# Two transformer blocks on one core: the GEMM units beside a stage's end split by token halves, and weights in half-MB pieces

## The reference

```python
def rmsnorm_2(x, g):
    y = xf * lax.rsqrt(jnp.mean(xf * xf, axis=-1, keepdims=True) + RMS_EPS)
    return (y * g.astype(jnp.float32)).astype(x.dtype)
...
for i in range(DEPTH_2):
    mod = c_act @ ada_w[i] + ada_b[i]
    sh1, sc1, g1, sh2, sc2, g2 = jnp.split(mod, 6, axis=-1)
    h = modulate(rmsnorm_2(x, norm_gain[i, 0]), sh1, sc1)
    y = mixer(h)          # swa, gla or fox, by i
    x = x + g1[:, None, :] * y
    h = modulate(rmsnorm_2(x, norm_gain[i, 1]), sh2, sc2)
    x = x + g2[:, None, :] * swiglu(h, ffn_w_gu[i], ffn_w_down[i])
```

## Time and profile before

| | |
|---|---|
| time, median of 3 runs | 2488.33 us (2488.05 to 2489.48) |
| the profiled execution | 2488.01 us |
| its span, first to last instruction | 2486.2 us |
| PE, DVE, ACT busy | 2277.7, 1615.7, 1097.2 us |
| mean granted clock of PE | 0.956 |
| read from memory | 450.30 MB, mean 184 GB/s |

### The profile page before, as it was taken

One profiled execution on the slowest core, in us unless ns is written; L12 is line 12 of the kernel. 1 busy time (PEld: TensorE's weight loads), 2 busy tenths in 40 slices (PEclk: granted clock), 3 DMA queues, 4 the chain that ended last, 5 costly groups with the idle time before them and its releaser, 6 DMA issues. The chain is left out here.

```text
span 2486.2 us, 34298 instructions
## 1 busy us (share of the span) xinstructions
PE 2277.7 (92%) x14225; PEld 2033.1 (82%) x14225; DVE 1615.7 (65%) x2293; ACT 1097.2 (44%) x1769; POOL 180.0 (7%) x183
## 2 busy tenths in 40 slices
PE   6999998989999998877999897999899999878998
PEld 6998886879988877756999775899786899757997
DVE  4676678656766785576888476777546555565554
ACT  4454445434444454444343442444444444444443
POOL 0000001010000011000000022000000000100000
PEclk8999999999999999878999998999998999988999
DMA  8866655556666654333899441587531465422551
GB/s 278 276 222 222 225 193 182 206 198 225 220 217 216 220 203 155 123 119 125 286 314 325 143 126 61 190 287 272 174 102 34 140 195 186 142 71 91 184 186 49
DMA packets 291919, 458.82 MB, mean 185 GB/s; under 512 B 10912, under 2 KB 158858, under 8 KB 291764
## 3 DMA queue, kind: packets, MB, share of 16 engines
q1 hardware_dynamic: 285796, 439.62, 52.5%
q0 software_dynamic: 5968, 17.02, 2.4%
HBM read 450.30 MB, written 6.29 MB: 184 GB/s over the span
## 5 line engine op out<-in xcount | busy, mean ns | idle before, releaser
L147 DVE TENSOR_TENSOR wlo<-raw,whi 128x1024 fp32r<-128x1024 f32 x640 | 775.0, 1236 | 405.9 <-ACT whi L141 404.4
L141 ACT ACTIVATE whi<-raw 128x1024 fp32r<-128x1024 f32 x640 | 662.2, 1055 | 532.0 <-PE G L135 496.1
L135 PE MATMUL G<-HTh,whi 128*128 128x256 f32 x2432 | 699.5, 288 | 6.8 <-DVE wlo L147 2.0
L135 PE MATMUL G<-HTl,whi 128*128 128x256 f32 x2432 | 690.0, 284 | 0.0
L135 PE MATMUL G<-HTh,wlo 128*128 128x256 f32 x2432 | 689.9, 284 | 0.0
L135 PEld LDWEIGHTS G<-HTh,whi 128*128 128x128 f32 x2432 | 468.4, 193 | 13.5 <-issue 7.4
L135 PEld LDWEIGHTS G<-HTl,whi 128*128 128x128 f32 x2432 | 468.5, 193 | 2.2
L135 PEld LDWEIGHTS G<-HTh,wlo 128*128 128x128 f32 x2432 | 468.2, 193 | 0.0
L135 PE MATMUL G<-whi,HTh 128*128 128x512 f32 (+1 forms) x704 | 278.3, 395 | 5.5 <-DVE pool L147 5.1
L155 DVE SCALAR_TENSOR_TENSOR pool<-raw,c,pool 128x512 f32<-128x512 f32 x336 | 267.9, 797 | 10.2
L135 PE MATMUL G<-wlo,HTh 128*128 128x512 f32 (+1 forms) x704 | 268.8, 382 | 0.0
(11 more groups left out here) (150 smaller groups left out, 2577.7 us busy)
## 6 DMA issues: line engine op xcount, KB each, us to landing
raw<-in_ada_w SPq DMA_DIRECT2D x96, 1024.0 KB, 5.9
raw<-in_ffn_w_gu SPq DMA_DIRECT2D x176, 512.0 KB, 4.9
raw<-in_w_in SPq DMA_DIRECT2D x112, 512.0 KB, 4.6
raw<-in_w_in SPq DMA_DIRECT2D x48, 1024.0 KB, 5.1
raw<-in_ffn_w_down SPq DMA_DIRECT2D x44, 1024.0 KB, 5.0
raw<-in_swa_w_in SPq DMA_DIRECT2D x12, 1024.0 KB, 5.2
raw<-in_gla_w_in SPq DMA_DIRECT2D x12, 1024.0 KB, 6.5
raw<-in_fox_w_in SPq DMA_DIRECT2D x12, 1024.0 KB, 5.3
```

The costliest lines, as they stand in the source:

```text
L135: return self.e.matmul(out, a, b, start=start, stop=stop, skip_group_check=True) if self.e else self
L141: return self.e.activation(out, a, func, bias=bias, scale=scale, accum_out=accum) if self.e else self
L147: return self.e.tensor_tensor(out, a, b, op) if self.e else self
```

## The change

The unit before each turn from one stage to the next, and the first unit of the next stage, are computed one token half after the other (`Apart`, six matmuls of 512 columns a step), and `turn` writes out their order: the first half of the last unit, its second half but for the last step, norm and transposes of the first half around that step, three steps of the next unit, norm and transposes of the second half around the fourth, then its second half. At the end of the FFN the last two down products take the place of the last unit. The scaling by the norm is applied to the rows on ACT (`rows`), and the transposes are plain; they go 4 blocks of 128 columns at a time, with four affine instructions of 128. The mean and power are made for each half, without the division by the width; the gains carry its root (32) instead. The first unit of each stage is one whose tokens are stationary (V first in the dilated, gla and fox stages), and the FFN's first gate/up unit is made that way too, with its own transposes. Weight pieces are 0.5 MB, with 8 raw buffers, 7 split slots and 5 halves ahead. Sums of ada pieces wait until six GEMM steps have passed. The last store goes in four parts.

```diff
-NRAW = 6
-NSPL = 5
-LOOK = 3
+NRAW = 8
+NSPL = 7
+LOOK = 4
...
-        self.raw = sb("raw", [P, NRAW, 4, 512])
+        self.raw = sb("raw", [P, NRAW, 2, 512])
...
-    return [("w", key, cseg(w, k * 512, 4, segs)) for k in range(K // 512)]
+    return [("w", key, cseg(w, k * 256, 2, segs)) for k in range(K // 256)]
...
+    add(("dil", l, 0, 3), wi, D, [g("lv", 0), g("lv", 1)])
...
-        for u in range(6):
+        for u in (2, 0, 1, 3, 4, 5):
...
-        for u in (0, 2, 4, 1, 3, 5):
+        for u in (4, 0, 2, 1, 3, 5):
...
+    def refill(self, n=LOOK + 1):
+        while len(self.halves) < n and self.held + len(self.halves) < NSPL and self.piece < len(self.stream):
+            self.fetch()
...
+    def ada_sums(self, age=6):
+        while self.adaq and self.steps - self.adaq[0][4] >= age:
+            l, u, b, acc, _ = self.adaq.pop(0)
...
+    def rows(self, dst, src, r, waits):
+        done = [self.new("ac_xn"), self.new("ac_xn")]
+        for c in range(2):
+            self.h_rows(dst[:, c * 512:c * 512 + 512], src[:, c * 512:c * 512 + 512], r, waits, done[c])
+        return done
...
+    def affine(self, t, c, g, tr, scol, bcol, ctok, hn=False):
+        tmp, have = self.mk_blk(2), self.new("ac_tr" if c else "ve_tr")
+        self.h_affine(g, tmp, c, hn, scol, bcol, tr, ctok, have)
+        self.gfree[g] = [have]
+        return tmp, have
...
+    def to_T(self, src, ready, dst, scol=None, bcol=None, const=1.0, ctok=(), nk=8, hn=False):
+        for t in range(2):
+            for c in range(nk // 4):
+                g, tr = self.tr4(src(t)[:, c * 512:c * 512 + 512], ready[t][c])
+                tmp, have = None, tr
+                if scol is not None:
+                    tmp, have = self.affine(t, c, g, tr, scol, bcol, ctok, hn)
+                self.split_tr(t, c, g, dst, tmp, have, const)
+        return [tr]
...
+    def turn(self, last, sums, make, head):
+        head.ahead = False
+        for f in last[0]:
+            f()
+        for f in last[1][:-1]:
+            f()
+        sums(0)
+        part = make(0)
+        a = part(0)
+        last[1][-1]()
+        b = part(1)
+        a[0]()
+        sums(1)
+        a[1]()
+        b[0]()
+        b[1]()
+        self.ada_sums(2)
+        part = make(1)
+        n = head.steps
+        for i in range(n - 1):
+            head(0, i)
+        a = part(0)
+        head(0, n - 1)
+        b = part(1)
+        for f in (a[0], b[0], a[1], b[1]):
+            f()
+        for i in range(n):
+            self.refill()
+            head(1, i)
+    def normed(self, scol, bcol, ctok):
+        def make(t):
+            q, have = self.mean(t, self.xsq)
+            self.refill(4 + t)
+            r, tr = self.rstd(q, have)
+            xn = self.mk_blk(4)
+            done = self.rows(xn.a, self.M.X[:, t, :], r, [tr] + self.xtok[t] + xn.w)
+            self.xtok[t] = self.xtok[t] + [done[1]]
+            def part(c):
+                g, tr = self.tr4(xn.a[:, c * 512:c * 512 + 512], [done[c]])
+                if c:
+                    xn.release([tr])
+                keep = []
+                return (lambda: keep.extend(self.affine(t, c, g, tr, scol, bcol, ctok)),
+                        lambda: self.split_tr(t, c, g, self.HT, *keep))
+            return part
+        return make
...
+        y_of(("ya", l, 0), 0, D, 0, gbs[0], False)
+        ya = y_of(("ya", l, 1), 0, D, 1, gbs[1], False)
...
+        def merge(t):
+            self.refill(4 + t)
+            def part(c):
+                g, tr = self.tr4(mg[:, t, c * 512:c * 512 + 512], [mtok[(t, c)]])
+                if t and c:
+                    merged.release([tr])
+                return (lambda: None), (lambda: self.split_tr(t, c, g, HT, None, tr, 0.5))
+            return part
+        self.turn(ya.both(), lambda t: None, merge, self.apart(HT, ("wo", l, 0), resid(0)))
+        last = self.apart(HT, ("wo", l, 1), resid(1))
...
+            make = self.modulated(0, 0)
+            head = self.swa_head(0)
+        self.turn(last.both(), sums, make, head)
...
+        def part(t, v, ns, first=False):
+            def f():
+                for kc in range(2):
+                    if (v, kc) not in ws:
+                        ws[(v, kc)] = self.take(("dn", l, v))
+                    n, lo = ws[(v, kc)]
+                    b = 2 * (v % 4) + kc
+                    done = ("pe_dn", (l, t, v, ns, kc))
+                    self.h_down1(t, ns, b, n % NSPL, lo, v == 10 and kc == 1, done)
+                    if t == 1 and ns[-1] == 1:
+                        self.give(n, done)
+                        OT.free[b] = [done]
+                if v == 10:
+                    fr = []
+                    for u in ns:
+                        fr += self.residual(gb, u, t, M.AB[t][:, u, :], done, nx, sq, n4)
+                    self.slots[t].ps_free = fr
+                    if t:
+                        gb.release(nx[0] + nx[1])
+            return f
+        last = ([part(0, 9, (0, 1)), part(1, 9, (0,)), part(0, 10, (0, 1))],
+                [part(1, 9, (1,)), part(1, 10, (0, 1))])
...
+            make = self.modulated(l, 1)
+            last = self.apart(self.OT, ("wo2", l, 1), ev(1))
+            self.turn(last.both(), sums, make, self.ffn_head(l))
...
+    def __call__(self, t, i):
+        o = self.o
+        if t == 0:
+            self.ns.append(o.take(self.key, self.ahead))
+        if i == 0:
+            self.g = o.gbank()
+        n, lo = self.ns[i]
+        done = (("pe_first", "pe_w")[t], n)
+        o.h_mm1(self.A, 2 * i, n % NSPL, lo, t, self.g, i == 0, i == 3, o.gfree[self.g], done)
+        if t:
+            o.give(n, done)
+            for b in (2 * i, 2 * i + 1):
+                self.A.free[b] = [done]
+        if i == 3:
+            o.gfree[self.g] = self.evac(t, o.M.GB[self.g], done)
+        o.step()
```

More of the change, by code:

```diff
@@ L403, in __init__ @@
         self.stream = weight_stream(M.I)
-        self.piece, self.half, self.halves, self.adaq = 0, 0, [], []
+        self.piece, self.half, self.halves, self.adaq, self.held, self.steps = 0, 0, [], [], 0, 0
         self.raw_free = [[] for _ in range(NRAW)]
@@ L554, in gemm @@
             end = kk == nk - 2
-            n, lo = self.take(key, ahead=not (last and end))
+            n, lo = self.take(key)
             used, first = ("pe_w", n), ("pe_first", n)
             self.h_mm(A, b0 + kk, n % NSPL, lo, modes, gs, kk == 0, end, [self.gfree[g] for g in gs], used, first)
-            self.spl_free[n % NSPL] = [used]
+            self.give(n, used)
             if end and modes == "TT":
@@ L1082, in swa_layer @@
         self.deferred.pop()()
+        self.ada_sums(0)
         self.widen(4)
@@ L1234, in ffn @@
             if v == 1:
                 gb = self.bcast(l * 48 + 40, M.mod, [self.mod_tok[l]])
[L1236 removed]
+            if v < 10:
                 down(v - 1)
[L1239 to L1247 removed]
@@ L1252, in ffn, with sums @@
         self.xsq = n4, sq
-        gb.release(nx)
+        def sums(t):
+            self.xtok[t] = nx[t] + sq[t]
+        make = self.modulated(l + 1, 0)
+        self.turn(last, sums, make, (self.swa_head, self.gla_head, self.fox_head)[(l + 1) % 3](l + 1))
     def run(self):
@@ L1358, in h_mm, with h_mm1 @@
         mm.then_inc(*self.up(used))
+    def h_mm1(self, A, kb, s, lo, t, g, start, end, free, done):
+        e, M = self.e, self.M
+        e.wait_ge(*self.at(lo))
+        if start:
+            for x in free:
+                e.wait_ge(*self.at(x))
+        for i in range(2):
+            for x in A.tok[kb + i][t]:
+                e.wait_ge(*self.at(x))
+            a = (A.hi[:, kb + i, t * P:t * P + P], A.lo[:, kb + i, t * P:t * P + P])
+            mm = self.three(M.GB[g][:, :], a, (M.whi[:, s, i, :], M.wlo[:, s, i, :]), start and i == 0, end and i == 1)
+        mm.then_inc(*self.up(done))
     def h_ada_sum(self, g, b, acc, free, summed, m, done):
@@ L1810, in h_foxgate, with h_gu0, h_gu @@
         self.soft_log(fb.a[:, 64:96], ("ve_log", "fox"), "fox")
-    def h_gu(self, part, ps, full, tmp, tanh, gated, u, dst, hi, lo):
+    def h_gu0(self, ps, tmp, act, full, free, tanh, gated, u):
+        e = self.e
+        e.wait_ge(*self.at(full))
+        for t in tmp.w:
+            e.wait_ge(*self.at(t))
+        e.activation(tmp.a[:, 0:256], ps[:, 0:256], ACT.Tanh, scale=0.5).then_inc(*self.up(tanh))
+    def h_gu(self, part, ps, full, tmp, tanh, gated, u, dst, hi, lo, end):
         e, OT = self.e, self.OT
@@ L2169, in h_foxgate, with h_gu0, h_gu @@
         e.tensor_scalar(z8, z, -8.0, None, ALU.mult).then_inc(*self.up(tz8))
-    def h_gu(self, part, ps, full, tmp, tanh, gated, u, dst, hi, lo):
-        e = self.e
+    def h_gu0(self, ps, tmp, act, full, free, tanh, gated, u):
+        e, g = self.e, tmp.a[:, 0:256]
+        e.wait_ge(*self.at(tanh))
+        e.scalar_tensor_tensor(g, g, 1.0, ps[:, 0:256], ALU.add, ALU.mult).then_inc(*self.up(gated))
+        e.wait_ge(*self.at(gated))
+        for t in free:
```

(8 more changed lines are left out.)

596 lines of the change are left out of this document (334 added, 262 removed).

## The result

The changed kernel takes 2572.18 us (median of 4 runs) beside 2488.6 for the kernel before on the same chip: ratio 1.0336, 95% interval 1.0318 to 1.0354. It is slower, as forecast, but by 84 us and not by 47, and outside the range.

A forecast was written before the change was run, and what follows sets the result against it. TensorE (PE) bounds the kernel, so only its stops and low clock count. Turns +49.7, outside them +15, won back 18: +46.7 on the profiled 2488.0 gives 2535 us, range 2470 to 2565.

The forecast's parts named there:

- the first stop of wo2 to FFN: Turn from wo2 to FFN: half 0's chain of 4.2 us is covered by three steps of half 1, 4.1 us.
- The FFN turns: Turns from FFN to next layer: 23.5 us against 13.2, +10.3 twice, and +9.2 to swa; 30 us.
- Rival 1: Deeper ring frees the queues, winning attention idle time and clock: 76 us instead of 10, total 2469; chance 0.20.
- Rival 2: Shorter stops in the turns do not lower the clock, saving 51 us: 2484, the same; chance 0.12.
- the two ya-to-wo turns: Turns from ya to wo: stops 2.0 and 2.95, clock 3.4, 10.1 us against 6.3, +3.8 each.
- Rival 3: Transfers bind: half-sized pieces make packets 1.2 times as long, the shallower ring cannot hide it; +25, 2560; chance 0.08.
- Rival 4: Halves starve: the seven split slots run dry at every turn, 1.5 us more each, 2550; chance 0.06.
- the gains of 18 us: Won back: 8 us from other waits for ada sums, 10 us of attention idle time from seven split slots.
- Three turns: The wo2-to-FFN turns other than the first: 14.5 us against 11.3, +3.2 each, 9.6 together.
- gla with one unit less beside its heads: In gla, one unit less hides attention steps, so its last two stages come uncovered: +4 us.
- The losses to the clock: In the turns, half clock loses 2.3 us after a stop near 5 us, 1.7 after one of 3 to 4.
- Setup and memory's second norm: Transposes with an affine go one group at a time through one block, 10.8 us for four: +9.

The follow-up runs named there:

- the next one: Half 0's affine-ahead kernel, with half 1's first four column blocks also scaled and split ahead of the head unit's fourth step: 2504.47 us, ratio 1.0073.
- the stream alone: Kernel before with only the change's weight stream (half-MB pieces, deeper ring, ada sums six steps late), no turn touched: 2481.75 us, ratio 0.9981.
- The fillers: Changed kernel with unused identity transposes (14, 20, 14) put into the stops of all eleven turns: 2543.85 us, ratio 1.0226.
- The fillers in the kernel before: Kernel before with 32 unused identity transposes ahead of the first diagonal matmul of each norm: 2488.67 us, ratio 1.0011.

## Why the prediction was off

**Right: the mechanism and its place.** PE bounds the kernel, and the loss is in its stops and the clock behind them. Which stops the new order makes, what ends them and how long they last was read off the queues before the change was built, and every entry of the table but the first stop of wo2 to FFN agrees within 1.1 us. That the affine waits for half 1's square was the cause named; the order with half 0's affine ahead confirmed it, and the next one did so for the third stop. The affine of four pieces was put at 1.3 us and measured 1.37. The FFN turns, the largest term, came to +9.2 for the first against +10.3. Rival 1 (queues get free) is refuted: its 76 us were 5. Rival 2 (the clock stays up) too, with 307 us at 1.2 GHz instead of 222, but for the two ya-to-wo turns, where it held. Rival 3 is refuted: the Trainium skill ("DMA: Bandwidth & Descriptors", section Bandwidth) wants DMAs of at least 1 MiB, by a table for transfers that GpSimd issues; here SyncE issues them. In this case pieces of 256 KB land in 4.6 us, those of 512 KB in 4.6 before, and the stream alone made the kernel 5 us faster; the rule did not decide here. Rival 4 did not show: splits were in time in the turns, they only stood in the way of others.

**Wrong, first: the gains of 18 us.** "ScalarE sat 496.1 us in front of a split" was read as a cost with a share that comes back. It was idle time of an engine that waits for PE in any case. The stream alone measured all these gains at 5 us net, with +5 in one attention stretch.

**Wrong, second: the first stop of wo2 to FFN**, 0.1 forecast, 1.9 to 4.2 measured, three lo splits ahead of the residual. The sum counted each operation of half 0's chain, and not what half 0's own takes put into VectorE's queue ahead of it. Three turns cost +21.0 instead of +9.6. Of the 11.4 us more, 6.7 are this stop itself; that the rest is the clock behind it is likely and not shown by itself.

**Wrong, third: cover.** gla with one unit less beside its heads was put at +4 and measured +9; fox's +3 was not in the sum. The step counted two uncovered stages; taking V's four k steps from the heads, and nothing else, measured 8 us in the runs.

**Mis-sized: clock and small norms.** The losses to the clock were taken as 1.7 to 2.3 us for each stop, 51 us in all. The fillers took 28 us off and left the order of the work as it was, so the losses are at least that; PE's products took 32 us less. Whether 51 was right in the sum the runs don't say; in places it was not: 3.4 us were put down for each ya-to-wo turn, where the clock stayed at 1.00 and the +3.8 each did not come. The fillers in the kernel before won 1.7 to 2.0 us at each wo2 turn and nothing at the FFN's ends, so the old turns, too, paid for the clock in some places only. Setup and memory's second norm were +13.2, not +9, and 9 of it memory's, most of that the order of its groups.

## What to carry over

When work is cut in halves so that one hides the other, write down each engine's queue in the new order and look for the first half's late steps behind the second half's early ones: here two reorderings were worth some 65 us. Count with them the prefetch work that the halves trigger, and the cover that a moved unit takes from others. Idle time of an engine that waits for the bottleneck is no reserve. Filling stops to keep the clock up was worth 28 us in one order of the work and nothing in the others, so it has to be measured turn by turn. And the total of a run can hide what an edit won in its place: put the traces side by side at equal work before calling an edit useless.

## What the runs showed of the hardware

The same code can have either clock. In the fox attention of the kernel before, the clock was 0.63 for 25 us; with only gla's order changed, the like stretch had 0.91, and the attention took 5.7 us less, though PE stood 2 us longer in it. Stops of PE of 1.76 and 2.31 us left the clock at 1.00 in the changed kernel's ya-to-wo turns. The kernel before spread from 2478 to 2494 us over the study, with mean clocks between 0.954 and 0.964, so that effects under 5 us needed the intervals. Transposes of the identity, 128x128 fp32, take 0.12 us each in the mean, and with them the granted clock of the windows around was higher (0.93 instead of 0.80 in the FFN's turn to gla), although they compute nothing.
